# Leaving out products of constants in the mixer and ahead of the second feed forward

## The reference, cut to what matters

```python
for l in range(DEPTH):                      # DEPTH = 2
    h = layer_norm(ALPHA * h + 0.5 * swiglu(h, ffn1...[l]), ln1...[l])
    mix = hybrid_mixer(h, ...)              # delta rule + convolution + latent attention, gated, @ w_out
    h = layer_norm(ALPHA * h + mix, ln2...[l])
    h = layer_norm(ALPHA * h + 0.5 * swiglu(h, ffn2...[l]), ln3...[l])
```

## Time and profile before

| | before |
|---|---|
| median of 3 runs | 3158.2 us (3149.61 to 3164.65) |
| the profiled execution's own time | 3149.56 us |
| its span, first to last instruction | 3147.8 us |
| TensorE MATMUL busy | 2997.1 us, 95% of the span, 16078 instructions |
| VectorE busy | 1887.3 us, 60% |
| ScalarE busy | 1364.4 us, 43% |
| mean granted TensorE clock | 0.981 of full |

### The profile page before, as it was taken

The page is one execution under the profiler, slowest core; times in us unless marked ns, Lnnn a source line. Parts: engine busy times, 40 slices in busy tenths (PEclk is TensorE's granted clock), DMA queues, the critical chain, the costliest instruction groups (busy, mean ns, idle before and its releaser), DMA issues.

```text
span 3147.8 us, 42901 instructions
## 1 busy us (share of the span) xinstructions
PE 2997.1 (95%) x16078; PEld 2469.9 (78%) x16078; DVE 1887.3 (60%) x2391; ACT 1364.4 (43%) x1562; POOL 46.9 (1%) x93
## 2 busy tenths in 40 slices
PE   8999999999999999889999999988999999999998
PEld 7997886599899878767988699454877887788776
DVE  6755632377677464326670454153887788778876
ACT  4431321144444122213531244132676667666765
POOL 2000010000000000000000000000000000000000
PEclk9999999999899999999999999998999999999999
DMA  8753321387577433126753365323999999999995
GB/s 285 240 180 138 134 81 55 107 267 243 195 260 241 146 117 107 56 80 228 253 187 107 134 199 169 117 76 109 358 328 320 341 338 328 320 340 339 328 321 211
DMA packets 375931, 659.69 MB, mean 210 GB/s; under 512 B 11626, under 2 KB 197848, under 8 KB 375832
## 3 DMA queue, kind: packets, MB, share of 16 engines
q1 hardware_dynamic: 375832, 658.32, 60.3%
HBM read 657.23 MB, written 1.05 MB: 209 GB/s over the span
## 4 chain that ended last, share of the span: by engine, by line
PE 76%; DVE 8%; issue 6%; ACT 4%; PEld 2%; DVEq 2%; DMA 1%; PEldq 1%; ACTq 1%; SPq 0%
PE banks L669 16%; PE banks L670 15%; PE banks L671 15%; PE banks L1143 9%; PE banks L1961 3%; PE banks L1993 3%; PE banks L1327 2%; PE banks L665 2%; DVE expert_rest L1069 2%; PE banks L742 1%; DVE ffn_arena L1008 1%; PE banks L1208 1%; PE banks L829 1%; DVE mod_sum L1001 1%; PE banks L841 1%
## 5 line engine op out<-in xcount | busy, mean ns | idle before, releaser
L669 PE MATMUL banks<-ffn_arena 128*128 128x256 f32 (+1 forms) x3460 | 1169.1, 338 | 46.2 <-DVE ffn_arena L1029 14.0
L671 PE MATMUL banks<-ffn_arena 128*128 128x256 f32 (+1 forms) x3460 | 1149.8, 332 | 0.0
L669 PEld LDWEIGHTS banks<-ffn_arena 128*128 128x128 f32 x3460 | 661.8, 191 | 123.8 <-issue 38.7
L1069 DVE TENSOR_TENSOR expert_rest<-expert_raw,ffn_arena 128x2048 fp32r<-128x2048 f32 (+1 forms) x306 | 646.2, 2160 | 118.5 <-ACT ffn_arena L928 117.4
L671 PEld LDWEIGHTS banks<-ffn_arena 128*128 128x128 f32 x3460 | 661.7, 191 | 69.1
L670 PE MATMUL banks<-ffn_arena 128*128 128x256 f32 (+1 forms) x2200 | 673.7, 306 | 0.0
L928 ACT ACTIVATE ffn_arena<-expert_raw 128x2048 fp32r<-128x2048 f32 (+1 forms) x306 | 538.6, 1815 | 113.7 <-PE banks L671 111.7
L670 PE MATMUL banks<-expert_rest,ffn_arena 128*128 128x512 f32 (+1 forms) x1224 | 465.9, 381 | 0.0
L670 PEld LDWEIGHTS banks<-ffn_arena 128*128 128x128 f32 x2200 | 424.7, 193 | 17.5 <-issue 0.5
L1143 PE MATMUL banks<-HT,panel 128*128 128x256 f32 x1280 | 281.1, 380 | 2.5 <-issue 2.5
L1143 PEld LDWEIGHTS banks<-HT,panel 128*128 128x128 f32 x1280 | 242.2, 190 | 37.5 <-issue 5.3
(11 more groups left out here) (401 smaller groups left out, 2777.9 us busy)
## 6 DMA issues: line engine op xcount, KB each, us to landing
expert_raw<-in_moe_w_gate_dram SPq DMA_DIRECT2D x90, 1024.0 KB, 5.2
expert_raw<-in_moe_w_up_dram SPq DMA_DIRECT2D x90, 1024.0 KB, 5.4
expert_raw<-in_moe_w_down_dram SPq DMA_DIRECT2D x90, 1024.0 KB, 5.1
gate_w<-in_ffn_w_gate_dram SPq DMA_DIRECT2D x55, 1024.0 KB, 5.4
up_w<-in_ffn_w_up_dram SPq DMA_DIRECT2D x55, 1024.0 KB, 5.4
down_w<-in_ffn_w_down_dram SPq DMA_DIRECT2D x55, 1024.0 KB, 5.4
mod_unit<-in_mod_w_dram SPq DMA_DIRECT2D x48, 1024.0 KB, 5.2
panel<-in_w_in_dram SPq DMA_DIRECT2D x24, 2048.0 KB, 7.8
```

What stands on the lines that cost most here:

```text
L669: mm(out, w[0], x[0], start=start, stop=False)
L671: return mm(out, w[1], x[0], start=False, stop=stop)
L1069: tt(rest[:, half, :], tile[:, half, :], high[:, half, :].bitcast(F32), ALU.subtract).then_inc(expert_lo, 1 if h else 1 + skipped)
```

## The change

Four calls go: the six products at L1362, the ten at L1429, the four in `turn_h` (by leaving its argument at 0) and the two before the second feed forward. No wait, no transfer and no other instruction changes. That is 22 products a layer, 44 in all.

```diff
@@ mixer_pe
             pe.drain().then_inc(panel_used, 1)
 
-            spin(3, 6)
             pe.wait_ge(o_ready, l + 1)
@@ mixer_pe
             pe.wait_ge(v_taken, l + 1)
-            spin(3, 10)
             pe.wait_ge(prob_ready, l + 1)
@@ the layer loop of TensorE
                 mixer_pe(pe, l)
-                turn_h(pe, l * 6 + 4, fill=4)
-                spin(0, 2)
+                turn_h(pe, l * 6 + 4)
                 ffn_pe(pe, n + NS, l * 2 + 1)
```

## The result

The changed kernel takes 3163.8 us (median of 20 runs, 3158.1 to 3171.1) against 3155.4 us (20 runs) before: 0.25% slower, ratio 1.0025, 95% interval 1.0014 to 1.0035, so 7.9 us, between 4.4 and 11.0. The sign was forecast; the size (17.5 us, 0.55%) was over twice what it is. The profiled execution took 3159.16 us against 3149.56 us.

A forecast was written before the change was run, and what follows sets the result against it. TensorE, busy for 95% of a 3147.8 us span, was taken to bound the kernel. Terms 2 x 2.8 + 2 x 4.2 + 3.5 = 17.5 us, added to 3158.2 us, gave 3175.7 us, range 3162 to 3189 us.

The forecast's parts named there:

- the six: Removed products at L1362: transpositions +0.7 us and L1327 +2.1 us at half clock, 2.8 us a layer (2.2 to 3.6).
- the ten: Removed products at L1429: 12 transpositions +1.2 us, the rest in the products with the values or L1327; 4.2 us a layer.
- No product lay on the path: At all four calls VectorE ends the wait later than the products end, so removing them gains 0.
- the 3.1 to 5.7: Microseconds that half clock lasts once dense work is back; 4.3 us was taken as the middle.
- the second tile's transpositions: Ahead of the second feed forward: at half they end 0.7 us later, hidden by VectorE's L1029 with 0.45 us of cover.
- the four and the two: Products removed before the second feed forward: it starts at half, 3.5 us over both layers (2.2 to 5.7).
- slower by over 0.5%: Outcome for the whole kernel: a slowdown of more than 15.8 us, given chance 0.62.
- if they bring the clock back: Second place: products with the values restore the clock as dense work does, L1327 runs at full; 3.3 us a layer.
- the share that I kept for L1327: Second place: if the products with the values don't restore the clock, L1327 pays 2.1 us too, 5.8 us a layer.
- the row of transpositions at 831.8: Earlier trace: clock 0.53 over 831.8 to 835.6, almost only transpositions, then 0.87; read as transpositions bringing the clock back.
- the clock is back sooner: Rival: transpositions count as clock work; first place 1.6 us, second 1.75 us a layer, 10.2 us in all; chance 0.18.
- the last sentence of the prediction: Prediction is wrong if, among others, falls elsewhere come or go by more than two or three, each 1.5 to 2.9 us.

The follow-up runs named there:

- e4: Changed kernel's three places, with each removed product replaced by two one-column products; ratio 1.0029 to the kernel before, 9.1 us slower.
- e1: Kernel before with only the six products at L1362 removed; ratio 1.0014, 4.4 us slower.
- e2: Kernel before with only the ten products at L1429 removed; ratio 1.0034, 10.7 us slower.
- e3: Kernel before with only the four and the two products ahead of the second feed forward removed; ratio 1.0006, 1.9 us slower.
- e5: The changed kernel measured again, on another run's chip; ratio 1.0020 to the kernel before, 6.3 us slower.
- e9: Changed kernel with the ten products at L1429 put back; ratio 1.0018 to the kernel before, 5.7 us slower.
- e6: Kernel before with twelve products instead of six at L1362 and twenty instead of ten at L1429; ratio 1.0069, 17 to 27 us slower.
- e7: Kernel before with five products instead of ten at L1429; ratio 1.0010, 3.2 us slower.
- e8: Kernel before with more constant products in other waits, at the feed forwards, L1390 and three shorter mixer waits; ratio 0.9987, 4 us faster.
- e10: e8 with two more products ahead of the attention scores, behind the wait for `v_taken`; ratio 0.9974 to the kernel before, 8.2 us faster, 3146.2 us.

## Why the prediction was right in sign and wrong in size

**Right.** No product lay on the path; VectorE ends all four waits; the clock is at half behind all three places in both layers; transpositions and dense products cost what was read from the earlier trace rows (0.9 for 0.7, 1.3 for 1.2, half a microsecond for each at half); half clock lasted 3.6 us in the feed forward and 3.9 us in L1327 (516.56 to 520.5) once the dense work was back, and 3.8 to 4.6 us in L1327 in the other stretches without the six, within the 3.1 to 5.7; the second tile's transpositions are hidden. e4 shows that the array's work was what held the clock.

**What failed** is the size of three terms of the sum: 17.5 us became 9.8, of which the four and the two make 3.5, the ten 2.6 and the six 1.6. The sizes measured are those of the traces, single executions; the times of e1, e2 and e3 alone would leave room for the terms as they were. The time, 3163.8 us, lies just inside 3162 to 3189 us, but that is no success of the sum: the change itself, 7.9 us, lies below its lower end, 12.0, and "slower by over 0.5%" had the larger chance.

**The term "the four and the two", 3.5 us, was about 0.** This step failed. The cost of a start at half was read from one pair of feed forwards, 191.1 against 189.0 us, though half of 3.5 us at half is 1.75, and the wait for the up weights' low part behind it was 1.9 to 2.7 us long. That wait takes a part of the loss up: it is 1.33 us in both layers now. Over the profiled executions whose second feed forwards I read, those without the products (changed, e3, e4, e5, e9) take 189.6 to 192.3 us, on average 190.1, and those with them (before, e1, e2) 188.9 to 191.0, on average 190.0. The 189.0 that I had compared with is one of two (188.9 in e1) in which the clock never fell, and four of the six with the products had a fall at their own first wait. (e6 and e7, which keep the four and the two as well, take 188.9 to 190.4 us, with such a fall in two of four.) So a start at half still costs about 0.9 us against a feed forward without any fall (189.9 on average over the nine that have no second fall, against 189.0), and what makes the term vanish is the other part: the fall behind the first wait stood in six of ten with the products and in one of ten without (e9, 192.3 us). The prediction had given this exchange to layer 0 alone, and at half its worth.

**The term "the ten", 4.2 us a layer, was 2.9 in the traces.** Transpositions +1.26, the products with the values +1.7 on average over eight stretches (0 twice, 1.8 to 2.6 six times), and nothing in L1327. The case "if they bring the clock back", 3.3 us, was nearly right, and the share that I kept for L1327 was wrong: the values' products themselves bring the clock back, or it is back before them (576.11, at full). For this the row of transpositions at 831.8 had been the right witness.

**The term "the six", 2.8 us a layer, is 2.7 to 3.2 where it stands,** and about 1.0 less in the end, because the next fall, 20 us later, mostly doesn't happen. The sum allowed for such shifts only in the feed forward, though the last sentence of the prediction names falls elsewhere as what could upset it.

The three corrected terms give 2 x (3.0 - 1.0) + 2 x 2.9 + 0 = 9.8 us; measured are 7.9 us (4.4 to 11.0) and 6.3 us (2.5 to 9.8). The sum is put together after the fact from the same traces, so that it fits is no test of it.

**The rival "the clock is back sooner"** had 10.2 us, close to what was measured, but by luck. Its mechanism fails at the first place: the clock came back at 520.5, 7.3 us after the transpositions began and not 4.3, and the place cost 2.7 to 3.2 us where the rival had 1.6. It holds at most at the second, where the clock was back within 4.5 us of their start in two of eight stretches. And it kept the 3.5 us for the four and the two.

**Open.** The ten alone measured 10.7 us, and adding them back to the changed kernel (e9 against e5) gained nothing that shows. The traces give 5.8. Falls among the scores, 4.6 us each and more, stood in 3 of 8 stretches without the ten (changed, e2, e4, e5) and in 5 of 12 with them (before, e1, e3, e6, e8, e9), so one profiled execution of each kernel can't say whether the ten's removal makes them likelier. The pair of executions shown above has one in layer 1 of the changed kernel (5.1 us) and none before, so its 9.6 us are not the change alone. That they carry a good part of the spread between runs is a guess: e10, in whose trace there is none, has the smallest. It was not shown run by run.

## What to carry to other kernels

Work whose result nobody reads can be off the path and still pay, if it stands in a wait and the engine's clock depends on its load; ask then not whether it is covered but what runs behind the wait, at which clock, and whether a later wait swallows the loss. Price a slower start by following it to the next wait that something else ends, not by comparing two whole stages once. And a remedy in one place moves the falls in the next, so judge several places together, and put the filler where traces show the falls: here fifteen more products a layer, in the mixer and at the feed forwards' starts, gained 8 us (5.4 to 11.0), about what leaving out 22 had cost.

## What the runs showed of the hardware

- Being busy is not enough for the clock. It fell at 565.6 in the midst of 40 one-column instructions without a pause (561.9 to 567.3), and at 511.0 though 24 of them had run to 510.1 (e4).
- It also fell among the scores, at 554.8 in e3, after 2.6 us of small products without a pause and with more of them following. Whether the 1.05 us wait ahead of them has a part in it is open: each of the nine such falls seen has that wait, and in e10, where two products fill it, there was none in two layers.
- Transpositions at half take 1.97 us for 8 and 2.79 us for 12, against 1.09 and 1.53 at full: 1.8 times. In layer 0 of the changed kernel the clock was back behind 12 of them alone, with full clock at 576.1 (so in 2 of the 8 stretches without the ten, the other being in e2). The Trainium skill ("TensorE: Matmul & The Clock Gate", Part 4, PE-mode transpose) says that the full clock doesn't engage for them, as they don't count as busy the same way; this trace, as the earlier trace rows, speaks against that.
- Falls seem to displace each other: the fall at L1390 stood in 9 of 10 stretches with the six products ahead of it and in 3 of 10 without, and the fall behind a second feed forward's first wait in 6 of 10 with the four and the two ahead of it and in 1 of 10 without.
